# Adding an output bias to the residual on GpSimd instead of in TensorE's accumulators

## The chip, the cores and the metric

The kernel runs on one NeuronCore of a Trainium2 chip. The metric is device time of one execution in microseconds. TensorE (PE) multiplies, VectorE (DVE), ScalarE (ACT) and GpSimd (POOL) work element by element, and SyncE (SP) issues most transfers. The engines run their own instruction streams and meet at semaphores.

## What is computed

Two blocks on 256 tokens of width 1024. The first is a token mixer and a mixture of experts. The second, which the change touches, has four layers; layers 0 and 3 ("banded", kind 0) use sliding-window attention with biases, layer 1 a dilated one and layer 2 a block one, both without biases:

```python
for i in range(DEPTH_2):                       # 4 layers, kinds 0, 1, 2, 0
    kind, j = i % N_MIXERS, i // N_MIXERS
    if kind == 0:
        h = mixer_a(x, a_w_qkv[j], a_b_qkv[j], a_sinks[j], a_w_o[j], a_b_o[j], cos, sin)
    ...
    x = layer_norm(DN_ALPHA * x + h, ln_g[i, 0], ln_b[i, 0])
    x = layer_norm(DN_ALPHA * x + swiglu(x, w_gate_up[i], w_down[i]), ln_g[i, 1], ln_b[i, 1])

def mixer_a(x, w_qkv, b_qkv, sinks, w_o, b_o, cos, sin):
    ...
    return o.reshape(B, S, nq).astype(x.dtype) @ w_o + b_o
```

The bias in question is `b_o` (1024 numbers per banded layer), so that layer's first residual is ALPHA x + o w_o + b_o.

## The kernel before

x lies in SBUF as two token tiles of 128 rows and 1024 columns (`x[:, t, :]`, tile name `rs`). All weights stream from HBM through `ring` in units of 128x1024, each used once; ScalarE copies a unit to `high` (L1185) and VectorE subtracts to get `low` (L1654), both in the matmul's rounded fp32 type, so that each product is three matmuls (high x high, high x low, low x high). A unit is used on TensorE only when `low_done` has counted it.

A banded layer runs like this. TensorE turns x (L531) for the projections. It projects values, keys and four quads of queries, ScalarE takes each result out of PSUM (`pg`) and VectorE applies the rope (L2155 to L2159). Scores go to `pd`, VectorE masks them (L2175), ScalarE takes exponents (L1545), VectorE the reciprocal (L2201), and GpSimd multiplies them in (`weigh`, L369). `weighted_values` transposes (L1052 to L1054) and gathers; ScalarE writes the high part of the attention output (`oth`, L1558), VectorE the low part (`otl`, L2208, semaphore `otl_out`).

The output projection accumulates in the four banks of `pd`, one for each token tile and half of the columns. In a banded layer, four products of a row of ones and the bias row (L1128, fp32, each two instructions) open these accumulators; then `wo_part(n, t)` adds unit n (of 8) for tile t in six matmuls. Units 0 to 3 are done for both tiles, then come `weighted_values` for the third quad, units 4 and 5 for tile 0, `weighted_values` for the last quad, units 6 and 7 for tile 0 (semaphore `wo_first`), and units 4 to 7 for tile 1. VectorE, when `wo_first` has come, computes ALPHA x + `pd` (`residual`, L1960), statistics (L1964), and the normalisation (L1999, L2000), and TensorE turns the new x for the feed-forward.

`gb` holds two rows broadcast to all partitions. In a banded layer GpSimd first loads the bias into row 0 and the norm's offset into row 1 (L428, L429). When TensorE has used the bias (`bo_used`), GpSimd loads the norm's gain into row 0 (L380), between the third and the fourth `weigh`. Nearly all matmuls go through one helper, `mm` (L443), so the trace tells them apart by tile: `pd<-gb,ones` are the bias matmuls and `pd<-high,oth` and the like the projection.

## Time and profile before

| | |
|---|---|
| median of 3 runs | 2270.2 us (2267.29 to 2271.64) |
| the profiled execution | 2268.9 us, span 2267.1 us |
| TensorE busy | 2121.1 us (94%) |
| VectorE, ScalarE, GpSimd busy | 1281.1, 920.1, 109.2 us |
| mean granted TensorE clock | 0.969 |

Times in the trace count from the span's start. A row's "idle before" is the time its engine stood still ahead of it, with what released it. The granted clock is a share of TensorE's full speed: 1.00 is 2.4 GHz and 0.50 is 1.2 GHz. TensorE's matmuls overlap, so that one's duration is longer than the distance between two starts.

### The profile page before, as it was taken

The numbers are of one execution on the slowest core, as the hardware profiler recorded it, in microseconds if no ns is written. First come the engines' busy times: TensorE is split into PE (matmuls) and PEld (weight loads), VectorE is DVE, ScalarE is ACT, GpSimd is POOL, SyncE is SP. The second block draws the span as 40 slices with busy tenths as digits, with TensorE's granted clock in tenths as the row PEclk, the third lists the DMA queues.
The fourth block names the chain that finished last, engine by engine and source line by source line (L and its number), as shares of the span: only waits on it lengthen the run. The fifth ranks groups of instructions, "written<-read, shape, count | busy, mean of one in ns | idle before, by whom it ended". The sixth has DMA issues, their size and how long they took to land.

```text
span 2267.1 us, 27822 instructions
## 1 busy us (share of the span) xinstructions
PE 2121.1 (94%) x11438; PEld 1701.7 (75%) x11438; DVE 1281.1 (57%) x1890; ACT 920.1 (41%) x1452; POOL 109.2 (5%) x115
## 2 busy tenths in 40 slices
PE   6999999989999988999999998999998999988997
PEld 2468767857888775788898896788796788866886
DVE  3346723245555574655677784755685655747554
ACT  2233340015444444444335554444463544444442
POOL 1000000000000001000001111000011000020000
PEclk9999999999999998999999998999999999989999
DMA  8142444434555441555443441555443555423551
GB/s 348 39 185 78 178 149 148 185 121 167 186 186 186 167 168 66 185 186 184 163 174 131 149 149 57 186 186 185 168 149 112 186 186 186 168 77 145 183 182 74
DMA packets 47118, 357.36 MB, mean 158 GB/s; under 512 B 5370, under 2 KB 5541, under 8 KB 9680
## 3 DMA queue, kind: packets, MB, share of 16 engines
q1 hardware_dynamic: 41904, 336.61, 41.0%
q0 software_dynamic: 4800, 18.50, 2.4%
q8 instruction: 91, 1.49, 0.3%
q10 hardware_dynamic: 288, 0.47, 0.1%
q14 instruction: 35, 0.29, 0.0%
HBM read 354.51 MB, written 1.05 MB: 157 GB/s over the span
## 4 chain that ended last, share of the span: by engine, by line
PE 85%; DVE 9%; ACT 3%; issue 1%; DMA 1%; POOL 0%; SPq 0%; DVEq 0%; ACTq 0%
PE pg L443 55%; PE pd L443 24%; PE pm L443 2%; PE pm L908 1%; DVE small L1964 1%; DVE low L1654 1%; DMA ring<-in_wstream 1%; DVE rs L2000 1%; DVE rs L1999 1%; DVE rs L1960 1%; DVE ar L2175 1%; DVE ar L1758 1%; ACT ar L1545 1%; PE pm L1052 1%; DVE xs L2010 1%
## 5 line engine op out<-in xcount | busy, mean ns | idle before, releaser
L1654 DVE TENSOR_TENSOR low<-ring,high 128x1024 fp32r<-128x1024 f32 x512 | 622.8, 1236 | 355.2 <-ACT high L1185 354.9
L443 PE MATMUL pg<-high,xs 128*128 128x512 f32 (+1 forms) x2496 | 745.2, 376 | 24.8 <-DVE xs L2010 14.3
L1185 ACT CAST high<-ring 128x1024 fp32r<-128x1024 f32 x512 | 525.0, 1049 | 368.0 <-PE pd L443 165.5
L443 PEld LDWEIGHTS pg<-high,xs 128*128 128x128 f32 x2496 | 460.9, 193 | 113.9 <-issue 22.1
L443 PE MATMUL pg<-low,xs 128*128 128x512 f32 (+1 forms) x1248 | 465.6, 373 | 0.0
L443 PE MATMUL pd<-high,hid 128*128 128x512 f32 x960 | 311.7, 396 | 7.0 <-DVE hid L2089 7.0
L443 PEld LDWEIGHTS pg<-low,xs 128*128 128x128 f32 x1248 | 240.5, 193 | 40.4
L443 PE MATMUL pg<-xs,high 128*128 128x256 f32 x1344 | 242.0, 283 | 0.0
L443 PEld LDWEIGHTS pd<-high,hid 128*128 128x128 f32 x960 | 180.6, 188 | 50.5 <-DVE hid L2089 8.2
L443 PEld LDWEIGHTS pg<-xs,high 128*128 128x128 f32 x1344 | 206.0, 188 | 5.0 <-issue 4.7
L443 PE MATMUL pg<-rh,ring 128*128 128x256 f32 (+1 forms) x832 | 203.9, 404 | 0.0
L443 PEld LDWEIGHTS pg<-rh,ring 128*128 128x128 f32 x832 | 159.7, 194 | 42.6 <-issue 22.5
L443 PE MATMUL pd<-low,hid 128*128 128x512 f32 x480 | 189.5, 395 | 0.0
L443 PE MATMUL pg<-xs,low 128*128 128x256 f32 x672 | 189.1, 281 | 0.0
L443 PEld LDWEIGHTS pg<-xs,low 128*128 128x128 f32 x672 | 126.5, 188 | 0.0
L443 PEld LDWEIGHTS pd<-low,hid 128*128 128x128 f32 x480 | 90.3, 188 | 21.0
L369 POOL TENSOR_TENSOR ar<-ar,small 128x256 f32<-128x256 f32 (+1 forms) x64 | 82.9, 1323 | 433.1 <-DVE small L2201 432.9
L2089 DVE TENSOR_TENSOR hid<-pm,hid 128x512 fp32r<-128x512 f32 x60 | 41.5, 691 | 92.3 <-ACT hid L1477 92.3
L1477 ACT CAST hid<-pm 128x512 fp32r<-128x512 f32 x60 | 35.2, 586 | 124.0 <-PE pm L908 124.0
L1545 ACT ACTIVATE ar<-ar,small 128x257 f32<-128x257 f32 (+5 forms) x128 | 67.0, 525 | 41.5 <-DVE small L2195 30.1
L1486 ACT ACTIVATE ar<-pg 128x256 f32<-128x256 f32 x120 | 46.2, 386 | 84.5 <-PE pg L443 84.4
L2155 DVE TENSOR_TENSOR ar<-ar,ropes 128x512 f32<-128x512 f32 x42 | 36.9, 880 | 68.4 <-ACT ar L1524 42.7
(333 smaller groups left out, 2007.8 us busy)
## 6 DMA issues: line engine op xcount, KB each, us to landing
ring<-in_wstream SPq DMA_DIRECT2D x256, 1024.0 KB, 4.8
ring<-in_wstream SPq DMA_DIRECT2D x31, 2048.0 KB, 7.8
gb<-in_long_rows POOLq DMA_DIRECT2D x21, 512.0 KB, 4.6
hdec<-in_hy_decay POOLq DMA_DIRECT2D x4, 512.0 KB, 6.6
rh<-in_xt SPq DMA_DIRECT2D x1, 1024.0 KB, 11.8
rh<-in_ctx SPq DMA_DIRECT2D x1, 1024.0 KB, 20.1
cx<-in_cx_tables POOLq DMA_DIRECT2D x1, 1024.0 KB, 5.0
cx<-in_dft_tables POOLq DMA_DIRECT2D x1, 1024.0 KB, 8.6
```

Of the source, the lines that this page charges most:

```text
L369: last = gp.tensor_tensor(w, w, smx[:, b, 2, t, 2 * p:2 * p + 2].unsqueeze(2).to_broadcast([P, 2, n]), ALU.mult)
L443: ins = nc.tensor.matmul(dst, lhs, rhs, start=start, stop=stop, skip_group_check=skip)
L908: last = nc.tensor.transpose(pm[u % 2][:, i * T + t * P:i * T + (t + 1) * P], hidden[:, t, i * P:(i + 1) * P], ident)
L1052: nc.tensor.transpose(pm[i][:, 0:P], scores(q, 0)[:, h, g * P:(g + 1) * P], ident)
L1185: nc.scalar.copy(high[:, (s - split0) % NHIGH, :], ring[:, s % NRAW, :]).then_inc(S("high_done"), 1)
L1477: nc.scalar.copy(hid[:, u % 2, 0, :, :], pm[u % 2][:, :].rearrange("p (i t) -> p i t", t=T)).then_inc(S("hid_high"), 1)
L1486: nc.scalar.activation(silu_g[:, t, :], pg[t][:, 0:T], ACT.Silu).then_inc(S("silu_done"), 1)
L1545: last = nc.scalar.activation(s, s, ACT.Exp, bias=smx[:, b, 0, t, h:h + 1], accum_out=smx[:, b, 1, t, h:h + 1])
L1654: V.tensor_tensor(low[:, s % NRAW, :], ring[:, s % NRAW, :], high[:, (s - split0) % NHIGH, :].bitcast(F32), ALU.subtract).then_inc(S("low_ ...
L1758: last = V.scalar_tensor_tensor(d, src, w[i], d, ALU.mult, ALU.add)
L2089: V.tensor_tensor(hid[:, u % 2, 1, :, :], pm[u % 2][:, :].rearrange("p (i t) -> p i t", t=T), hid[:, u % 2, 0, :, :].bitcast(F32), ALU.sub ...
L2155: V.tensor_tensor(rt[:, 0, :, :], raw[:, e % 2, :, :], cos.unsqueeze(1).to_broadcast([P, 2, T]), ALU.mult)
```

## The change

In banded layers GpSimd, after the first loads and after TensorE has turned x, scales each token tile of x by ALPHA in place and adds the bias row, then loads the gain into `gb` row 0, all ahead of its first `weigh`. TensorE's bias matmuls go, and `wo_part` opens the accumulators itself. VectorE's residual there is a plain add. In all four layers `wo_first` is now signalled twice, behind unit 6 and behind unit 7, and VectorE waits for the one whose half it adds.

```diff
--- before.py
+++ after.py
@@ -373,11 +373,17 @@
             def attention(layer):
 
                 kind, q0 = KINDS[layer], 4 * layer
+                if kind == 0:
+                    gp.wait_ge(S("bo_landed"), 16 * (layer // 3 + 1))
+                    gp.wait_ge(S("x_turned"), 4 * (2 + 2 * layer))
+                    for t in range(TT):
+                        gp.tensor_scalar(x[:, t, :], x[:, t, :], ALPHA, None, ALU.mult).then_inc(S("x_raised"), 1)
+                        gp.wait_ge(S("x_raised"), 2 * (layer // 3) + t + 1)
+                        gp.tensor_tensor(x[:, t, :], x[:, t, :], gb[:, 0, :], ALU.add).then_inc(S("bo_added"), 1)
+                    gp.wait_ge(S("bo_added"), 2 * (layer // 3 + 1))
+                    gp.dma_start(gb[:, 0, :], row_of(f"ln_g{2 * layer}")).then_inc(S("gains_landed"), 16)
                 for i in range(3):
                     weigh(q0 + i)
-                if kind == 0:
-                    gp.wait_ge(S("bo_used"), layer // 3 + 1)
-                    gp.dma_start(gb[:, 0, :], row_of(f"ln_g{2 * layer}")).then_inc(S("gains_landed"), 16)
                 weigh(q0 + 3)
 
             gp.memset(cs[:, :, :], 0.0).then_inc(S("cs_zero"), 1)
@@ -1123,12 +1129,6 @@
 
                 n0 = first[("wo", layer)]
                 pe.wait_ge(S("masked"), PROJ[q0 + 4])
-                if kind == 0:
-                    pe.wait_ge(S("bo_landed"), 16 * (layer // 3 + 1))
-                    for t in range(TT):
-                        for c in range(2):
-                            last = mm(pd[:, 2 * t + c, :], ones[0:1, :], gb[0:1, 0, c * 512:(c + 1) * 512], True, False)
-                    last.then_inc(S("bo_used"), 1)
 
                 def wo_part(n, t):
                     w = weights(n0 + n)
@@ -1137,7 +1137,7 @@
                         for l, r in ((0, 0), (0, 1), (1, 0)):
                             o = (k % 2) * 512
                             last = mm(pd[:, 2 * t + c, :], (oth, otl)[l][:, k, t * P:(t + 1) * P], w[r][:, o:o + 512],
-                                      kind > 0 and k == 0 and (l, r) == (0, 0), k == KT - 1 and l == 1)
+                                      k == 0 and (l, r) == (0, 0), k == KT - 1 and l == 1)
                     return last
 
                 pe.wait_ge(S("otl_out"), q0 + 2)
@@ -1153,8 +1153,7 @@
                 weighted_values(q0 + 3)
                 pe.wait_ge(S("otl_out"), q0 + 4)
                 for n in (6, 7):
-                    last = wo_part(n, 0)
-                last.then_inc(S("wo_first"), 1)
+                    wo_part(n, 0).then_inc(S("wo_first"), 1)
                 for n in range(4, 8):
                     wo_part(n, 1).then_inc(S("unit_used"), 1)
                 at[0] = n0 + 8
@@ -1949,13 +1948,15 @@
                 then(V.tensor_tensor(mix[:, m, :], mix[:, m, :], mtmp[:, 0, :], ALU.add))
                 V.tensor_tensor(mix[:, m, :], mix[:, m, :], mtmp[:, 1, :], ALU.add).then_inc(S("mixed"), 1)
 
-            def residual(t, h, mod=None):
+            def residual(t, h, mod=None, raised=False):
 
                 half = x[:, t, h * 512:(h + 1) * 512]
                 src = pd[:, 2 * t + h, :]
                 if mod is not None:
                     then(V.tensor_tensor(rtmp, src, gb[:, mod, h * 512:(h + 1) * 512], ALU.mult))
                     ins = V.tensor_tensor(half, half, rtmp, ALU.add)
+                elif raised:
+                    ins = V.tensor_tensor(half, half, src, ALU.add)
                 else:
                     ins = V.scalar_tensor_tensor(half, half, ALPHA, src, ALU.mult, ALU.add)
                 ins.then_inc(S("res_out"), 1)
@@ -2282,15 +2283,17 @@
                 low_output(q0 + 3)
                 split_to(w0 + 11)
                 n = 3 + 2 * layer
-                dve.wait_ge(S("wo_first"), layer + 1)
-                residual(0, 0)
-                residual(0, 1)
+                if kind == 0:
+                    dve.wait_ge(S("bo_added"), 2 * (layer // 3 + 1))
+                for h in range(2):
+                    dve.wait_ge(S("wo_first"), 2 * layer + h + 1)
+                    residual(0, h, None, kind == 0)
                 statistics(n, 0, False)
                 normalised(n, 0)
                 dve.wait_ge(S("unit_used"), w0 + 8 - split0)
-                residual(1, 0)
+                residual(1, 0, None, kind == 0)
                 low_part(n, 0)
-                residual(1, 1)
+                residual(1, 1, None, kind == 0)
                 statistics(n, 1, False)
                 normalised(n, 1)
                 low_part(n, 1)
```

## Rows read from the trace of the kernel before

**Rows 1.** the page's part 4, the whole span's chain, its shares by engine.
```profile
PE 85%; DVE 9%; ACT 3%; issue 1%; DMA 1%; POOL 0%; SPq 0%; DVEq 0%; ACTq 0%
```

**Rows 2.** the chain in order of time, layer 0's projection (start, us, what).
```profile
867.72 16.49 PE pd L443 x56
```

**Rows 3.** timeline, layer 0's projection (start, us, engine, what, idle before it).
```profile
865.38 0.30 PE L1052 MATMUL pm<-consts,ar 128*128 128x128 f32 x1 [2.05 <-ACT ar L1556]
...
867.65 3.69 PE L443 MATMUL pd<-gb,ones 1*128 1x512 f32 x8
...
868.39 0.69 DVE L2208 TENSOR_TENSOR otl<-pg,oth 128x512 fp32r<-128x512 f32 x1 [1.93 <-ACT oth L1558]
...
871.28 0.50 PE L443 MATMUL pd<-high,oth 128*128 128x512 f32 x1
...
888.20 0.69 DVE L2208 TENSOR_TENSOR otl<-pg,oth 128x512 fp32r<-128x512 f32 x1 [16.12 <-ACT oth L1558]
...
888.95 0.51 PE L443 MATMUL pd<-high,oth 128*128 128x512 f32 x1 [1.41 <-DVE otl L2208]
```

**Rows 4.** the same timeline in layer 3.
```profile
2019.83 0.69 DVE L2208 TENSOR_TENSOR otl<-pg,oth 128x512 fp32r<-128x512 f32 x1 [3.32 <-ACT oth L1558]
...
2023.21 0.80 PE L443 MATMUL pd<-high,oth 128*128 128x512 f32 x1
```

**Rows 5.** TensorE by stretch (stretch, us, busy, instructions, granted clock, DMA, GB/s).
```profile
867.70:871.30 3.60, 3.60 (x11) 1.00 0.02 5
...
871.90:875.30 3.40, 3.40 (x10) 0.50 0.41 154
875.30:884.00 8.70, 8.70 (x39) 1.00 0.36 121
...
2015.30:2018.70 3.40, 3.40 (x18) 0.51 0.03 10
...
2023.20:2029.00 5.80, 5.80 (x15) 0.50 0.24 90
```

**Rows 6.** VectorE's residual (L1960) and the turn of tile 0 behind it (L531).
```profile
899.81 0.69 DVE L1960 SCALAR_TENSOR_TENSOR rs<-rs,pd 128x512 f32<-128x512 f32 x1 [0.51 <-PE pd L443]
...
  PE pd L443: 4.6, 8
...
907.12 0.66 PE L531 MATMUL pm<-consts,rs 128*128 128x128 f32 x4 [0.80 <-DVE rs L2000]
```

**Rows 7.** GpSimd's groups by shape (busy us, mean ns of one, idle before).
```profile
L369 POOL TENSOR_TENSOR ar<-ar,small 128x1536 f32<-128x1536 f32 x8 | 27.2, 3404 | 0.0
...
L395 POOL MEMSET rs<- 128x3684 f32 x1 | 3.2, 3168 | 23.1 <-PE pd L443 23.1
```

**Rows 8.** GpSimd and VectorE at the start of layer 0; L428's landing times.
```profile
806.08 0.53 POOL L428 DMA_DIRECT2D gb<-in_long_rows  x1 [302.34 <-DVE rs L1997]
...
DMA to landing us min/median/max: 3.9/4.0/4.0
...
813.61 2.36 DVE L1654 TENSOR_TENSOR low<-ring,high 128x1024 fp32r<-128x1024 f32 x2 [0.54 <-ACT high L1185]
...
818.81 0.69 DVE L2155 TENSOR_TENSOR ar<-ar,ropes 128x512 f32<-128x512 f32 x1 [2.84 <-ACT ar L1529]
...
824.51 0.69 DVE L2155 TENSOR_TENSOR ar<-ar,ropes 128x512 f32<-128x512 f32 x1 [1.34 <-ACT ar L1529]
...
830.20 0.69 DVE L2155 TENSOR_TENSOR ar<-ar,ropes 128x512 f32<-128x512 f32 x1 [1.33 <-ACT ar L1529]
...
846.46 3.17 POOL L369 TENSOR_TENSOR ar<-ar,small 128x256 f32<-128x256 f32 x4 [39.33 <-DVE small L2201]
```

**Rows 9.** GpSimd and VectorE side by side in layer 1.
```profile
1212.69 3.60 DVE L1654 TENSOR_TENSOR low<-ring,high 128x1024 fp32r<-128x1024 f32 x2
...
1216.21 3.23 DVE L2155 TENSOR_TENSOR ar<-ar,ropes 128x512 f32<-128x512 f32 x1
...
1212.85 6.05 POOL L369 TENSOR_TENSOR ar<-ar,small 128x768 f32<-128x768 f32 x2 [3.78 <-DVE small L2201]
```

## Prediction

> **What bounds the kernel now.** I read the page's chain that ended last first: 85% of the span is TensorE, 9% VectorE [rows 1]. So time is won by taking work off TensorE, or by shortening a wait that TensorE stands in, and work on another engine is free as long as it stays beside TensorE. Then I followed the chain in order of time through layer 0's output projection: it runs through one unbroken stretch of 56 matmuls into `pd`, 16.49 us long [rows 2]. Eight of those 56 are the bias matmuls that the change removes; the other 48 are units 0 to 3 of the projection (four units, two token tiles, six matmuls each). GpSimd is not on that chain. Four views then carry the numbers: the timeline at the bias matmuls of layers 0 and 3 (what would TensorE wait for without them?), the granted clock by stretch around them, VectorE's idle time ahead of its residual, and what VectorE and GpSimd do to each other when both are busy.
>
> **Bias matmuls removed: the start of the projection.** In layer 0 the first bias matmul starts at 867.65 and the first projection matmul at 871.28 [rows 3]. The whole 3.63 us is not won. The projection also waits for VectorE's low half of the attention output (`otl_out`), which starts at 868.39, takes 0.69 and so ends at 869.08 [rows 3]. Where TensorE has nothing else to do it starts 0.06 after such an end (888.20 + 0.69 = 888.89, matmul at 888.95) [rows 3]. So the new start is 869.15 and the gain 2.13 us. TensorE stands idle for about 1.4 us instead. Layer 3: the same operation ends at 2019.83 + 0.69 = 2020.52, the new start is 2020.59 against 2023.21 [rows 4], gain 2.62 us. Together 4.75 us. `wo_part` now opens the accumulators itself with the start flag, which is no instruction. The wait on `bo_landed` leaves TensorE; it was long satisfied.
>
> **Bias matmuls removed: the clock.** The bias matmuls contract over a single row. The granted clock is 1.00 while they run in layer 0 (867.70 to 871.30), 0.50, the 1.2 GHz level, from 871.90 to 875.30, directly behind them, and 1.00 again from 875.30 [rows 5]. In layer 3 they also run at 1.00 and the projection behind them at 0.50 from 2023.20 to 2029.00 [rows 5]. What the engine did before each fall was to stream those single-row matmuls, though the trace counts it as busy. I take it that they let the clock fall as idling would, and that an idle gap of 1.4 us with full matmuls behind it does less harm than 3.6 us of them: in layer 0 the gap of 2.05 us before 865.38 [rows 3] had no fall behind it (1.00 from 867.70 on). It is no law: layer 3 is at 0.51 from 2015.30 to 2018.70, behind the same gap [rows 5]. A stretch at 0.50 does half the work of its length, so the two cost 3.4 / 2 = 1.7 us and 5.8 / 2 = 2.9 us, together 4.6 us. Bounds: 0 (it falls all the same) to 4.6. Since the clock moves with what lies around it and everything behind layer 0 shifts, I count one new stretch of 1.7 us at 0.50 somewhere and keep 2.9 us.
>
> **`wo_first` in two steps, all four layers.** VectorE may add the first half of tile 0 when unit 6 is done, not unit 7. In layer 0 it stood idle for 0.51 us before that add, waiting for TensorE [rows 6]; ahead of that it converts the last two weight units and can't be earlier. The add and its statistics then run beside unit 7's six matmuls, and the second half starts 0.5 us sooner. The idle time put down to TensorE ahead of this line is 4.6 us in 8 waits [rows 6]: one at the projection and one at the end of each of the four layers, and the change leaves the latter alone. I take the 0.51 for all four projections. The saving reaches TensorE, since it stands idle 0.80 us before the second turn of tile 0 for VectorE's normalisation [rows 6]. 4 x 0.51 = 2.0 us, bounds 1.3 (if the first turn, where it can gain only about 0.3, decided) to 2.0.
>
> **Work added on GpSimd.** Per banded layer two scalings and two adds, each 128x1024 f32. None of that size is in the trace. The adds: its multiplication takes 3.40 us at 128x1536 [rows 7], in proportion 3.40 x 1024 / 1536 = 2.3 us each. The scaling, one tensor in, is bounded below by a memset, 3.17 us for 3684 columns, so 0.9 us for 1024 [rows 7], and above by the add, 2.3; I take 1.2, near the memset, since its second operand is a constant. Per layer 2 x (1.2 + 2.3) = 7.0 us, bounds 6.4 to 9.2. GpSimd starts when `a_bo` has landed: issued at 806.08, about 4.0 to land [rows 8], so at 810.1, and ends near 817 to 821. The turns that read x are over by then. Queued behind it on GpSimd are the DMA of the gain (now in place some 50 us sooner, moved ahead of three `weigh` calls) and the first `weigh`, which before started at 846.46 [rows 8]. So 25 us of cover. Cost on GpSimd's own queue: nothing. Its `weigh` of the last quad no longer waits for TensorE; nobody was waiting for it.
>
> **What it does to VectorE.** In layer 1, with GpSimd at two multiplications for 6.05 us, VectorE's rope product took 3.23 us instead of 0.69, and two weight conversions 3.60 instead of 2.36 [rows 8, 9]. So VectorE lost 3.78 us in 6.05, or 0.62 per us of GpSimd's time. The Trainium skill, "SBUF — State Buffer", section "Who interferes with whom", says why: a VectorE instruction with two inputs in SBUF shares GpSimd's read interface, and the one that comes second waits for the whole of the other. The trace agrees: each of those instructions has two SBUF inputs. For this change 0.62 x 7.0 = 4.4 us of VectorE's time per banded layer, 5.7 at the upper bound. VectorE's idle time from there on is 0.54 + 2.84 + 1.34 + 1.33 = 6.05 us up to the rope at 830.20 [rows 8]. One projection of a quad lasts 824.51 - 818.81 = 5.70 us there, in which VectorE converts two units (2.36), so TensorE's units come with time in hand. So I cost it at 0, bounds 0 to 2 us per layer (the loss in one lump just before 818.81). If that cover were gone the price would be the 4.4. The same page gives no duration; the Trainium skill, "GPSIMD Engine Reference", section "2.1 Instruction dispatch", adds about 6 us for the first call of freshly loaded code. No run here shows it. By it GpSimd would end near 827, still 19 us before its next work, and the sum would stay.
>
> The residual itself becomes an add instead of a scale-and-add, with one input in PSUM as before: 0, both are one pass over 512 columns.
>
> **Sum.** 4.75 + 2.9 + 2.0 = 9.65 us. The profiled execution took 2268.9 us (span 2267.1), so 2259.3. It lies 1.3 us under the median of the three runs, 2270.2; against that the forecast is 2260.5.
>
> **Rivals.**
> (A) The clock falls all the same, since TensorE now idles for 1.4 us right behind the small gather matmuls. For: in layer 3 the clock is at 0.50 already in the stage before. Against: the projection begins 2.1 to 2.6 us sooner with full matmuls. Gain 4.75 + 2.0 = 6.8, time 2263.4. Chance 0.22.
> (B) GpSimd's work isn't hidden: VectorE's delay passes the idle time and reaches the score chain from 830 on, which has none to spare. 2 us per layer off the sum: gain 5.7, time 2264.5. With (A) as well, gain 2.8, time 2267.4. Together 0.13.
> (C) Slower. GpSimd's one-input scaling runs far above my bound, and each us of it takes 0.62 from VectorE. Per layer the loss must pass 6.05 us idle plus half of the 9.65 gain, 10.9 us, so GpSimd must be busy for 17.6 us per layer, or 6.5 us for each scaling; at 10 us each it is (24.6 x 0.62 - 6.05) x 2 - 9.65 = +8.8 us, time 2279. By the rows an operation on one input has no reason to cost thrice one on two. Chance 0.03.
> (D) The change doesn't do what it says: TensorE's saved time turns up as a wait for something later than `otl_out`, for instance converted weight units. Against: VectorE, which converts them, is idle for 16.12 us in that stage [rows 3], so all that could be converted was. Time 2269 or so. Chance 0.04.
> Forecast: 0.58.
>
> **Range and chances.** 80%: 2256.5 (both clock stretches kept, 4.6) to 2266.0 (A and B, part of their joint case left out). A measurement of this kernel can tell about 0.2%, 4.5 us, from no change, so faster means under 2265.7. That holds for the forecast, A, and B alone: 0.86. Same: B with A, and D, and a little of the spread: 0.11. Slower: C, 0.03.
>
> **What would show it.** Right: the first projection matmul starts 0.06 us after `otl`; no matmuls from `gb`; the granted clock is 1.00 over most of the 48 matmuls, which then take some 11 us; the 0.51 us idle before the residual is gone in all four layers; GpSimd's four operations at the start of layers 0 and 3 take 6.4 to 9.2 us in all, VectorE's conversions and ropes beside them are stretched, and TensorE has no new wait before 830. Wrong: the clock at 0.50 in the projection; TensorE waiting on VectorE in the projections of q or k; GpSimd's scaling above 2.3 us.

## The result, and the profile after

| | before | after |
|---|---|---|
| median of the runs made together (4 each) | 2268.74 us | 2254.91 us (2253.15 to 2257.61) |
| the profiled execution | 2268.9 us, span 2267.1 | 2257.61 us, span 2255.8 |
| TensorE busy | 2121.1 us | 2106.3 us |
| VectorE, ScalarE, GpSimd busy | 1281.1, 920.1, 109.2 us | 1291.1, 920.1, 133.6 us |

The ratio is 0.9939, with a 95% interval of 0.9922 to 0.9956: faster by 13.8 us. The forecast was 2260.5, with a range of 2256.5 to 2266.0. The direction was right, but the time lies 1.6 us under the range. So two questions are left: which term was too small, and whether the rest belongs to the change.

The page's part 4 of after, the chain's shares by engine, against [rows 1]:

```profile
PE 83%; DVE 10%; ACT 4%; issue 2%; DMA 1%; POOL 0%; SPq 0%; ACTq 0%; DVEq 0%
```

TensorE still bounds the kernel and GpSimd is still not on the chain, though it works 24 us longer. TensorE's timeline of after at layer 0's projection (start, us, engine, what, idle before it), against [rows 3]:

```profile
868.47 1.56 PE L449 MATMUL pg<-ar 128*64 128x256 f32 x16
871.49 0.47 PE L449 MATMUL pd<-high,oth 128*128 128x512 f32 x1 [1.46 <-issue]
...
2014.60 0.47 PE L449 MATMUL pd<-high,oth 128*128 128x512 f32 x1 [1.46 <-issue]
```

The last row is the projection's start in layer 3. VectorE's timeline in layer 0:

```profile
870.70 0.69 DVE L2209 TENSOR_TENSOR otl<-pg,oth 128x512 fp32r<-128x512 f32 x1 [1.93 <-ACT oth L1557]
```

Where eight bias matmuls ran, TensorE is idle for 1.46 us, in layer 3 as in layer 0, and the projection starts 0.10 us after VectorE's low half (870.70 + 0.69 = 871.39). The times are not those of [rows 3], since the execution before this point was 2.2 us longer, so from here on distances are compared. The granted clock around it, TensorE by stretch (stretch, us, busy, instructions, granted clock, DMA, GB/s), against [rows 5]; the last three rows are layer 3:

```profile
867.70:871.30 3.60, 2.33 (x22) 1.00 0.00 0
871.60:875.30 3.70, 3.70 (x17) 1.00 0.02 4
875.30:882.60 7.30, 7.30 (x33) 1.00 0.44 144
...
2014.60:2018.60 4.00, 4.00 (x17) 1.00 0.00 0
2018.70:2023.00 4.30, 4.30 (x20) 1.00 0.32 99
2023.20:2029.00 5.80, 5.47 (x40) 1.00 0.58 192
```

No stretch of either projection is at 0.50, the 1.2 GHz level. TensorE is less busy right ahead of the projection than before (2.33 of 3.60 us instead of 3.60), and the clock nonetheless stays at its 2.4 GHz level.

The last term, VectorE's first residual in layer 0, and the answer on the line of the residual for the other layers and the feed-forwards (idle time, times), against [rows 6]:

```profile
895.54 2.36 DVE L1653 TENSOR_TENSOR low<-ring,high 128x1024 fp32r<-128x1024 f32 x2 [0.25 <-ACT high L1184]
897.82 0.68 DVE L1959 TENSOR_TENSOR rs<-rs,pd 128x512 f32<-128x512 f32 x1
...
  PE pd L449: 2.6, 4
```

The 0.51 us of idle time is gone. Of 4.6 us in 8 waits, 2.6 us in 4 are left. But the residual now starts right behind the conversion of two weight units: what is late next is VectorE's own order of work.

GpSimd at the start of layer 0, against [rows 7] and [rows 8]:

```profile
813.20 3.77 POOL L380 TENSOR_SCALAR rs<-rs 128x1024 f32<-128x1024 f32 x1 [3.40 <-DMA gb<-in_long_rows]
817.05 2.64 POOL L382 TENSOR_TENSOR rs<-rs,gb 128x1024 f32<-128x1024 f32 x1
819.67 3.74 POOL L380 TENSOR_SCALAR rs<-rs 128x1024 f32<-128x1024 f32 x1
823.50 2.39 POOL L382 TENSOR_TENSOR rs<-rs,gb 128x1024 f32<-128x1024 f32 x1
...
848.77 1.60 POOL L369 TENSOR_TENSOR ar<-ar,small 128x256 f32<-128x256 f32 x2 [21.97 <-DVE small L2202]
```

The four operations take 3.77 + 2.64 + 3.74 + 2.39 = 12.5 us, not 7.0, and lie outside the bounds of 6.4 to 9.2. GpSimd still has 22 us of idle time before its first `weigh`. The 6 us that the prediction allowed for a first call didn't show: the first scaling started when the bias had landed and took 3.77 us, the second 3.74. VectorE beside it:

```profile
810.83 9.95 DVE L1653 TENSOR_TENSOR low<-ring,high 128x1024 fp32r<-128x1024 f32 x6 [0.32 <-ACT high L1184]
821.11 1.11 DVE L2156 TENSOR_TENSOR ar<-ar,ropes 128x512 f32<-128x512 f32 x1 [0.33 <-ACT ar L1528]
...
823.53 4.57 DVE L1653 TENSOR_TENSOR low<-ring,high 128x1024 fp32r<-128x1024 f32 x2
```

Undisturbed, two conversions take 2.36 us and the rope product 0.69 [rows 8]. So VectorE lost (9.95 - 3 x 2.36) + (1.11 - 0.69) + (4.57 - 2.36) = 5.5 us in 12.5, 0.44 per us of GpSimd instead of 0.62. The idle time ahead of these rows, 0.54, 2.84 and so on before, is down to 0.3 us each: the loss went into VectorE's idle time.

The table gives distances between starts of TensorE's matmuls, in us, for each kernel of the study. "Start" runs from the turn of tile 1 to the first projection matmul (in layers 0 and 3), "48" over the 48 matmuls of units 0 to 3 and the weighted values behind them, up to unit 4 (in after the 48 matmuls alone take 11.2 us of it), "end" from unit 6 to the turn of tile 0, "turns" from there to the turn of tile 1 in layer 0, "layer 1" from its turn of tile 1 to the first projection matmul and from there to unit 6.

| kernel | start 0 | 48 in 0 | end 0 | turns 0 | layer 1 | start 3 | 48 in 3 |
|---|---|---|---|---|---|---|---|
| before | 65.66 | 17.67 | 8.93 | 10.61 | 273.63 + 28.06 | 67.74 | 18.76 |
| after | 63.65 | 16.07 | 8.44 | 10.50 | 273.79 + 25.31 | 65.05 | 16.08 |
| e1 after again | 63.63 | 16.07 | 8.43 | 10.55 | 273.82 + 25.31 | 65.08 | 16.08 |
| e2 no bias | 63.63 | 16.07 | 8.94 | 10.60 | 273.78 + 27.85 | 64.95 | 16.07 |
| e3 full rows | 65.19 | 16.40 | 8.94 | 9.09 | 273.52 + 28.02 | 66.63 | 16.40 |
| e4 two steps | 65.79 | 17.59 | 8.44 | 10.53 | 273.63 + 28.04 | 67.20 | 17.67 |
| e5 GpSimd later | 67.47 | 16.08 | 8.43 | 8.96 | 276.50 + 27.90 | 69.01 | 16.07 |
| e6 GpSimd last | 65.16 | 16.07 | 8.44 | 10.52 | 273.86 + 25.30 | 64.98 | 16.08 |
| e7 no bias, two steps | 63.63 | 16.08 | 8.44 | 10.52 | 275.25 + 26.88 | 65.10 | 16.07 |
| e8 high first | 63.57 | 15.56 | 8.97 | 10.48 | 273.81 + 24.79 | 64.41 | 15.56 |
| e9 GpSimd long | 67.52 | 16.06 | 8.44 | 10.52 | 273.75 + 27.86 | 69.11 | 16.07 |
| e10 VectorE's order | 65.15 | 16.08 | 8.43 | 8.69 | 276.28 + 25.30 | 65.12 | 16.08 |
| e11 both orders | 62.05 | 15.56 | 8.46 | 8.87 | 276.28 + 24.78 | 64.42 | 15.57 |

From before to after the three terms of the sum are: start 65.66 - 63.65 = 2.01 and 67.74 - 65.05 = 2.69, together 4.70; clock 17.67 - 16.07 = 1.60 and 18.76 - 16.08 = 2.68, together 4.28; two steps 8.93 - 8.44 = 0.49, and about 0.50 in each of the other three layers, 2.0. That makes 11.0 us, or a ratio of 0.9951. It is within the measured interval, yet in layer 1, whose work on TensorE up to there is the same, the second part differs too, by 28.06 - 25.31 = 2.75 us. The distance between the two turns differs with the clock as well. It is 10.5 us where the granted clock over it is 0.84, and 9.0 where it is 1.00; in after it is 10.50, 8.97, 8.97 and 10.52 in layers 0 to 3, in before 10.61, 10.54, 9.08 and 10.62.

### The profile page after: what moved, and what is told of

It is laid out like the page before. It is cut to its first block, busy times and chain, and to the rows that moved or that the text cites. A ratio compares the mean times of both kernels' runs of the same rounds, so it can differ in the third digit from the quotient of the medians.

```text
span 2255.8 us, 27800 instructions
## 1 busy us (share of the span) xinstructions
PE 2106.3 (93%) x11422; PEld 1690.1 (75%) x11422; DVE 1291.1 (57%) x1890; ACT 920.1 (41%) x1452; POOL 133.6 (6%) x123
## 4 chain that ended last, share of the span: by engine, by line
PE 83%; DVE 10%; ACT 4%; issue 2%; DMA 1%; POOL 0%; SPq 0%; ACTq 0%; DVEq 0%
PE pg L449 55%; PE pd L449 23%; PE pm L449 2%; DVE low L1653 1%; PE pm L914 1%; DVE small L1965 1%; DVE rs L2001 1%; DVE rs L2000 1%; DMA ring<-in_wstream 1%; DVE ar L2176 1%; DVE rs L1961 1%; DVE ar L1757 1%; ACT high L1184 1%; ACT ar L1544 1%; PE pm L1058 1%
## 5 line engine op out<-in xcount | busy, mean ns | idle before, releaser
L1653 DVE TENSOR_TENSOR low<-ring,high 128x1024 fp32r<-128x1024 f32 x512 | 630.8, 1252 | 356.0 <-ACT high L1184 355.7
L449 PEld LDWEIGHTS pg<-high,xs 128*128 128x128 f32 x2496 | 458.2, 191 | 114.5 <-issue 21.7
```

What stands on the lines that cost most here:

```text
L449: ins = nc.tensor.matmul(dst, lhs, rhs, start=start, stop=stop, skip_group_check=skip)
L1653: V.tensor_tensor(low[:, s % NRAW, :], ring[:, s % NRAW, :], high[:, (s - split0) % NHIGH, :].bitcast(F32), ALU.subtract).then_inc(S("low_ ...
```

## The experiments

Each diff is against before or after, as said. The expectations stand as they were written ahead of the runs. The numbers are those of the table (e1 is the first experiment); the ninth is told ahead of the eighth.

### The changed kernel once more

No edit. The question is whether the time beyond the forecast comes again.

> The changed kernel as it is, for a second profile and a closer ratio. The first profile won 13.5 us from the first turn of layer 0 on: 11.0 us by the terms of my sum (4.7 start, 4.3 clock, 2.0 two steps) and 4.3 us in layer 1 (2.75 in its output projection, 1.6 at the turn behind it), where only the clock differed, less some given back elsewhere. Theory 1 (the clock's share in layer 1 is chance): the second profile has other places at 0.50, the terms of the sum measure 11 us again, and the ratio settles near 0.995 (2268.7 - 11 = 2257.7). Theory 2 (it is brought about by the change): layer 1's projection is at 1.00 again and the ratio stays at 0.9939.

Measured: 2254.17 us (2252.97 to 2255.56), ratio 0.9944 (0.9931 to 0.9957). The stretches of the table are those of the first profile within 0.05 us, layer 1's 25.31 among them. So the time is the kernel's own and not one lucky execution. One stretch outside the table is not the same: the turns of layer 3 are 8.96 us apart here and 10.52 in the first profile, so the clock can differ between two executions of one program. What the ratio can't say is whether all of it comes from the change's parts; the others below can.

### The bias left out, nothing else

Against before; the output bias is missing from the result, and GpSimd does nothing new.

```diff
-                    gp.wait_ge(S("bo_used"), layer // 3 + 1)
+                    gp.wait_ge(S("bo_landed"), 16 * (layer // 3 + 1))
...
-                            last = mm(pd[:, 2 * t + c, :], ones[0:1, :], gb[0:1, 0, c * 512:(c + 1) * 512], True, False)
...
-                                      kind > 0 and k == 0 and (l, r) == (0, 0), k == KT - 1 and l == 1)
+                                      k == 0 and (l, r) == (0, 0), k == KT - 1 and l == 1)
```

> The kernel before without the eight bias matmuls of each banded layer and with nothing in their place; the output bias is left out of the result. wo_first stays one signal, GpSimd adds nothing. My theory: the projection starts 2.1 and 2.6 us sooner, 0.06 us behind otl, and stays at a clock of 1.00, which gives 4.3 more: 9.0 us, 2259.7, ratio 0.9960. Rival A (the clock falls all the same while TensorE idles): 4.75 us, 2264.0, ratio 0.9979. Against the changed kernel it shows what GpSimd's work costs: 11.0 less 9.0 less 2.0 for the two steps, so nothing by my theory.

Measured: 2257.26 us, ratio 0.9958 (0.9942 to 0.9973), where 0.9960 was expected. "Start" falls by 2.03 and 2.79, "48" by 1.60 and 2.69: removing the bias matmuls gives 9.1 us by itself, and the start and clock terms are both theirs. (Layer 1 is 301.6 us here, as in before; what it gives in after is missing.)

### The same bias matmuls over all 128 rows

Against before: a stationary identity and the bias in all rows of `gb`. The arithmetic is the same, the number of instructions too.

```diff
-                            last = mm(pd[:, 2 * t + c, :], ones[0:1, :], gb[0:1, 0, c * 512:(c + 1) * 512], True, False)
+                            last = mm(pd[:, 2 * t + c, :], ident, gb[:, 0, c * 512:(c + 1) * 512], True, False)
```

> The kernel before, its bias matmuls with the identity as stationary operand and all 128 rows of the broadcast bias: same number, same columns, same type, all rows of the array instead of one. My theory (it is the single row that lets the clock fall): the bias matmuls take the same 3.6 us, the projection starts at the same place, but at a clock of 1.00 in both banded layers; 4.3 us won, 2264.4, ratio 0.9981. Rival (the clock falls for what lies ahead of them, the small transposes and gathers, or for their fp32 type): 0.50 behind them as before, ratio 1.000.

Measured: 2262.25 us, ratio 0.9978 (0.9967 to 0.9989); 0.9981 was expected, 1.000 by the rival. TensorE's timeline and its granted clock by stretch, of this kernel:

```profile
870.02 3.70 PE L443 MATMUL pd<-gb,consts 128*128 128x512 f32 x8
873.15 0.79 PE L443 MATMUL pd<-high,oth 128*128 128x512 f32 x1
...
867.70:871.30 3.60, 3.55 (x25) 1.00 0.02 5
871.60:875.30 3.70, 3.70 (x13) 1.00 0.00 0
875.30:882.60 7.30, 7.30 (x34) 1.00 0.48 174
...
2018.70:2023.00 4.30, 4.30 (x16) 1.00 0.09 25
2023.20:2029.00 5.80, 5.80 (x27) 1.00 0.37 121
```

The eight matmuls take 3.70 us as they did with a single row (3.69 in [rows 3]). But the projection behind them runs at 1.00, and "48" is 16.40 us in both layers instead of 17.67 and 18.76. The fourth experiment below keeps the single row and has the fall in both layers (17.59 and 17.67); the eight profiles that have 1.46 us of idle time in this place have none of it in 16 of 16. So the fall of the clock belongs to the single-row matmuls: the number of instructions, their columns and their time are unchanged (the stationary operand is an identity in place of ones as well, which no run varies by itself). That is 1.27 + 2.36 = 3.6 us of the clock term without removing an instruction; "start" is shorter too, by 0.47 and 1.11, the larger in layer 3, where the stage ahead ran at 0.51 before [rows 5]. The measured gain, 0.22%, is 5.0.

### The first residual in two steps, nothing else

Against before.

```diff
-                    last = wo_part(n, 0)
-                last.then_inc(S("wo_first"), 1)
+                    wo_part(n, 0).then_inc(S("wo_first"), 1)
...
-                dve.wait_ge(S("wo_first"), layer + 1)
-                residual(0, 0)
-                residual(0, 1)
+                for h in range(2):
+                    dve.wait_ge(S("wo_first"), 2 * layer + h + 1)
+                    residual(0, h)
```

> The kernel before with wo_first signalled behind unit 6 and behind unit 7, and nothing else. My theory: VectorE's 0.51 us idle ahead of the residual goes in four layers, and the turns behind it come 0.5 us sooner each: 2.0 us, 2266.7, ratio 0.9991. Rival (the turn of the first half waits for TensorE's own matmuls): 0.3 us in each layer, 1.3 us, ratio 0.9994. The distance from otl to the second turn in the profile tells them apart more closely than the times.

Measured: 2264.55 us, ratio 0.9991 (0.998 to 1.0002), as expected but not told from 1 by the time alone. The trace tells it: "end" is 8.44 in place of 8.93.

### GpSimd's work behind the first `weigh`

Against after. The same four operations and DMA, some 35 us later.

```diff
+                weigh(q0)
                 if kind == 0:
...
-                for i in range(3):
+                for i in (1, 2):
                     weigh(q0 + i)
```

> The changed kernel with GpSimd's scaling and add behind the first weigh of a banded layer, where VectorE's mask, maximum and rope steps are on the chain, instead of ahead of it. In the changed kernel's profile that work takes 12.5 us per layer (scaling 3.8, add 2.6 each), not my 7.0, and VectorE lost 5.6 us beside it, 0.45 us per us. My theory (it is free only where VectorE has idle time and GpSimd nothing due): the second weigh, due some 12 us behind the first, comes 4 us late, and VectorE loses up to 5.6 us on the chain: 3 to 6 us per banded layer, 6 to 12 us in all, ratio to the kernel before 0.997 to 1.000. Rival (GpSimd's place does not matter): 0.9944, as the changed kernel.

Measured: 2263.41 us, ratio 0.9978 (0.9967 to 0.999): the gain is more than halved. GpSimd, then VectorE, of this kernel in layer 0:

```profile
849.57 2.77 POOL L381 TENSOR_SCALAR rs<-rs 128x1024 f32<-128x1024 f32 x1
852.42 2.34 POOL L383 TENSOR_TENSOR rs<-rs,gb 128x1024 f32<-128x1024 f32 x1
854.74 3.21 POOL L381 TENSOR_SCALAR rs<-rs 128x1024 f32<-128x1024 f32 x1
858.03 2.87 POOL L383 TENSOR_TENSOR rs<-rs,gb 128x1024 f32<-128x1024 f32 x1
...
853.73 1.58 DVE L2157 TENSOR_TENSOR ar<-ar,ropes 128x512 f32<-128x512 f32 x1 [3.64 <-ACT ar L1529]
855.24 1.25 DVE L2158 SCALAR_TENSOR_TENSOR ar<-ar,ropes 128x256 f32<-128x256 f32 x1
...
857.47 4.51 DVE L1654 TENSOR_TENSOR low<-ring,high 128x1024 fp32r<-128x1024 f32 x2
```

Here the rope products (1.58 and 1.25 us) and the conversions (4.51 instead of 2.36) lie on the way to the scores, and VectorE's loss passes to TensorE: "start" is 3.82 us longer than in after in layer 0 and 3.96 in layer 3. Of each, 2.7 to 2.8 us are idle time of TensorE, the rest is its matmuls at a lower clock (0.53 and 0.57 from 8 to 4 us ahead of the projection, where after has 1.00 and 0.99). The 7.8 us together are close to the 8.5 by which the medians differ, but that hides more: in the profiles layer 1 is 5.3 us longer than in after (304.4 and 299.1) and layer 2 3.1 us shorter, in code that neither kernel changes. Rival B's mechanism is real; its place was wrong.

### GpSimd's work behind the last `weigh`

Against after: the `weigh` loop of all four quads is moved ahead of the block.

```diff
+                for i in range(4):
+                    weigh(q0 + i)
                 if kind == 0:
...
-                for i in range(3):
-                    weigh(q0 + i)
-                weigh(q0 + 3)
```

> The changed kernel with GpSimd's scaling and add behind the last weigh, beside the output projection, where VectorE has stood idle for 12 to 16 us. It measures the scaling without VectorE beside it. Theory 1 (my 1.2 us was right and the port shared with VectorE stretched it to 3.8): the scaling takes 1.0 to 1.5 us here, the add 2.3. Theory 2 (GpSimd's scaling is that slow by itself): 2.9 us or more. Either way it ends before the residual needs it, and the ratio is the changed kernel's, 0.9944 within 0.001.

Measured: 2253.54 us, ratio 0.9946 (0.9934 to 0.9958). GpSimd has nobody beside it here, so this is also the price of its operations alone. Its timeline in layer 0, and the answer on the scaling's line (min/median/max ns):

```profile
876.39 2.77 POOL L382 TENSOR_SCALAR rs<-rs 128x1024 f32<-128x1024 f32 x1
879.25 2.40 POOL L384 TENSOR_TENSOR rs<-rs,gb 128x1024 f32<-128x1024 f32 x1
...
L382 POOL TENSOR_SCALAR rs<-rs x4: 2768/2770/2773, 876.4 to 2020.9; 128x1024 f32<-128x1024 f32 x4
```

The scaling takes 2.77 us every time. So it is slow by itself, slower than the add of two tensors of that size (2.40), and sharing with VectorE adds 0.35 to 1.0 us (3.12 to 3.77 in after). The late place is as good as the early one. One stretch is worse, and GpSimd is not the cause of it: "start" in layer 0 is 65.16 instead of 63.65. The tenth experiment has it too (65.15), whose code up to there is that of after. TensorE's transposes ahead of the projection, first of after, then of the tenth:

```profile
867.69 0.30 PE L1058 MATMUL pm<-consts,ar 128*128 128x128 f32 x1 [2.38 <-ACT ar L1555]
```

```profile
866.09 0.40 PE L1058 MATMUL pm<-consts,ar 128*128 128x128 f32 x1 [1.84 <-ACT ar L1555]
...
871.47 0.48 PE L449 MATMUL pd<-high,oth 128*128 128x512 f32 x1 [1.46 <-issue]
```

From the first transpose to the projection it is 3.80 us in the one (to 871.49, above) and 5.38 in the other, and the transpose itself takes 0.30 and 0.40. From 860 to 870 the granted clock was 0.84 in after and 0.69 in the tenth. The same code runs there at another clock.

### The bias left out and the two steps: the change without GpSimd's work

Against before, the diffs of the second and the fourth experiment together; the output bias is missing.

> The kernel before without the bias matmuls and with wo_first in two steps; GpSimd does nothing for the bias, which is left out of the result. It is the changed kernel less GpSimd's work. My theory (that work is hidden): 11.0 us by the terms, ratio 0.9951, the same as the changed kernel within the interval. Rival (GpSimd's work costs TensorE time at the start of the banded layers): this kernel is the faster by up to 4 us, ratio 0.993 or less. The stretch from the turn of layer 0 to its first projection matmul, 63.65 us in the changed kernel, would be shorter here by the same.

Measured: 2255.16 us, ratio 0.995 (0.9939 to 0.9962), 0.9951 expected. Taking all of GpSimd's 25 us away brings nothing over after (0.9939 and 0.9944), and "start" is the same within 0.05 us (63.63 and 65.10 against 63.65 and 65.05). GpSimd's work costs nothing where the change put it. Layer 1 takes 275.25 + 26.88 = 302.1 us here, where before takes 301.7 and after 299.1.

### Three scalings where one is

Against after: two more scalings by 1.0 per tile, so that GpSimd is busy 23.8 us per layer. This is rival C's case, made on purpose.

```diff
-                        gp.tensor_scalar(x[:, t, :], x[:, t, :], ALPHA, None, ALU.mult).then_inc(S("x_raised"), 1)
-                        gp.wait_ge(S("x_raised"), 2 * (layer // 3) + t + 1)
+                        for i in range(3):
+                            gp.tensor_scalar(x[:, t, :], x[:, t, :], ALPHA if i == 2 else 1.0, None, ALU.mult).then_inc(S("x_raised"), 1)
+                            gp.wait_ge(S("x_raised"), 6 * (layer // 3) + 3 * t + i + 1)
```

> The changed kernel with three scalings of each tile on GpSimd instead of one (two of them by 1.0), so that its work per banded layer grows from 12.5 us to about 25. It asks where the cover ends and what a us beyond it costs, which is the price of my slower rival (C). By the prediction's rate, 0.62 us of VectorE per us of GpSimd less 6.05 us of idle time: 9.2 us per layer beyond the changed kernel, 18 in all, ratio 1.002 to the kernel before. By the rate of the changed kernel's profile, 0.45: 5 us per layer, 10 in all, 0.9988. If the idle time of VectorE up to the mask step hides it all: 0.9944.

Measured: 2264.34 us, ratio 0.9986 (0.9976 to 0.9995). By a rate of 0.45 it was to be 0.9988, by the 0.62 of the prediction 1.002. GpSimd and VectorE in layer 0:

```profile
812.74 9.35 POOL L381 TENSOR_SCALAR rs<-rs 128x1024 f32<-128x1024 f32 x3 [3.15 <-DMA gb<-in_long_rows]
822.18 2.69 POOL L383 TENSOR_TENSOR rs<-rs,gb 128x1024 f32<-128x1024 f32 x1
824.95 9.07 POOL L381 TENSOR_SCALAR rs<-rs 128x1024 f32<-128x1024 f32 x3
834.10 2.64 POOL L383 TENSOR_TENSOR rs<-rs,gb 128x1024 f32<-128x1024 f32 x1
...
834.42 2.88 DVE L2157 TENSOR_TENSOR ar<-ar,ropes 128x512 f32<-128x512 f32 x1
```

The rope at the head of the score chain waits inside GpSimd's last add (2.88 us instead of 0.69), and "start" grows by 3.87 and 4.06 us. Together that is 7.9 us of the 10 that the rate of 0.45 gives; that the ratio came so close is partly chance, since layers 1 and 2 again differ from after by 2.5 us more and 3.1 less. Some 11 us more of GpSimd in a layer cost 4 us there, so the cover of [rows 8] ends between 12.5 and 23.8 us of GpSimd's work.

### The projection's high parts first

Against after: at units 4 and 6 TensorE starts with the high part of the attention output, which ScalarE has ready before VectorE's low half; units 0 and 1 no longer wait for the second quad.

```diff
-                    for k in (2 * i, 2 * i + 1):
-                        for l, r in ((0, 0), (0, 1), (1, 0)):
+                    if opens:
+                        pe.wait_ge(S("oth_out"), q0 + i + 1)
+                    for l, r in ((0, 0), (0, 1), (1, 0)):
+                        if opens and l:
+                            pe.wait_ge(S("otl_out"), q0 + i + 1)
+                        for k in (2 * i, 2 * i + 1):
...
-                pe.wait_ge(S("otl_out"), q0 + 2)
+                pe.wait_ge(S("otl_out"), q0 + 1)
                 for n in range(4):
+                    if n == 2:
+                        pe.wait_ge(S("otl_out"), q0 + 2)
...
```

> The changed kernel with the output projection ordered so that TensorE waits less for the low half of the attention output: units 0 and 1, which need only the first quad, start without the second; and where a quad's first unit opens, the four matmuls with the high half run while VectorE makes the low half. My theory: the 1.4 us idle ahead of the projection in the two banded layers goes (2.8 us), and each of the eight waits of 1.41 us ahead of units 4 and 6 falls to 0.7 (5.6 us), together 8.4 us below the changed kernel, ratio to the kernel before 0.9907. Rival (VectorE's or ScalarE's later steps are then due and the turns behind the projection come no sooner): half of it, 0.9925.

Measured: 2252.23 us, ratio 0.9943 (0.9929 to 0.9958). Neither 0.9907 nor the rival's 0.9925 was met. TensorE's wait ahead of units 4 and 6 did get shorter (0.78 us instead of 1.41). TensorE's, then VectorE's timeline of this kernel:

```profile
883.02 0.70 PE L449 MATMUL pd<-high,oth 128*128 128x512 f32 x2 [0.78 <-ACT oth L1561]
...
890.99 2.36 DVE L1657 TENSOR_TENSOR low<-ring,high 128x1024 fp32r<-128x1024 f32 x2 [0.26 <-ACT high L1188]
893.27 0.68 DVE L1963 TENSOR_TENSOR rs<-rs,pd 128x512 f32<-128x512 f32 x1
```

The residual stands behind two conversions, as in after, and unit 6 being done sooner doesn't help it: "end" goes back from 8.44 to 8.97. In layer 1 the second part is 0.52 us shorter and "end" takes all of it back; in the banded layers 0.5 us of some 1.2 to 1.8 goes. The rest of the missing gain is not explained by this wait. In this profile the turns of layer 2 also stand 11.87 us apart at a clock of 0.71, where after has 8.97 at 1.00.

### VectorE's order around the residual

Against after: one of the two conversions is moved behind work that TensorE waits for.

```diff
-                split_to(w0 + 11)
+                split_to(w0 + 10)
...
                 low_part(n, 0)
+                split_to(w0 + 11)
```

> The changed kernel with VectorE converting only one of the last two weight units ahead of the residual and the other behind the low half of tile 0. In the profiles VectorE starts the residual 0.0 us behind the second conversion, so it is what stands ahead now. Theory: the residual starts up to 1.1 us sooner, held by unit 6 of the projection; the second turn's idle 0.75 us goes, in four layers: 3.0 us below the changed kernel, ratio 0.9931. Rival (TensorE is still busy with the projection of tile 1 then, and the late conversion delays tile 1's residual): no change, 0.9944.

Measured: 2251.58 us (2248.33 to 2252.29), ratio 0.9929 (0.9917 to 0.994); 0.9931 expected. "Turns" falls from 10.50 to 8.69. Most of that is the clock. TensorE over the turns of after in layers 0 and 1, then of this kernel in layer 0:

```profile
903.78:914.28 10.50, 8.45 (x33) 0.84 0.40 162
1417.18:1426.14 8.96, 6.92 (x33) 1.00 0.47 191
```

```profile
903.77:912.46 8.69, 7.06 (x33) 1.00 0.48 184
```

At the same clock of 1.00 the order of VectorE's work gives 0.28 us per layer, 1.1 in four, and not the 3.0 expected. The other 1.5 us each in layers 0 and 3 come from the clock. Both kernels with this order have all eight of their turns at 1.00, and the seven others with the two steps and the old order of VectorE and TensorE have 14 of 28 there, so the order may well be what keeps the clock up; no run isolates it. That the ratio came out as expected doesn't show that the reason was right.

### Both orders together

The edits of the last two experiments in one kernel.

> The order of e8 and the order of e10 together on the changed kernel. In e8 TensorE was 1.3 us per layer sooner at unit 6 but the turn came 8.97 us behind it instead of 8.44, since VectorE stood between. Theory: with VectorE's conversion out of the way the turn comes 8.35 us behind unit 6 and its second half without idle time: 5 to 8 us below the changed kernel, ratio 0.991 to 0.9925. Rival: the end of the projection is bound by the low half of the last quad alone, and it is e8's ratio, 0.9943.

Measured: 2246.17 us (2242.88 to 2248.34), ratio 0.9906 (0.9892 to 0.992). VectorE and TensorE in layer 0:

```profile
890.80 1.23 DVE L1657 TENSOR_TENSOR low<-ring,high 128x1024 fp32r<-128x1024 f32 x1 [0.26 <-ACT high L1188]
891.95 0.68 DVE L1963 TENSOR_TENSOR rs<-rs,pd 128x512 f32<-128x512 f32 x1
...
898.43 0.60 PE L537 MATMUL pm<-consts,rs 128*128 128x128 f32 x4
899.25 0.66 PE L537 MATMUL pm<-consts,rs 128*128 128x128 f32 x4 [0.22 <-DVE rs L2005]
```

One conversion instead of two stands ahead of the residual, "end" is back at 8.46, and the turns are 8.87 us apart in all four layers. By the ratios to before this version is 0.33% faster than the changed kernel, and faster than either reordering alone. How much of it is shorter waits and how much the clock, no run separates.

## Why the prediction was right and wrong

**The start of the projection: right.** 4.75 us forecast, 4.70 measured. The rule that carried it (the new start is the end of VectorE's low half plus what TensorE needs to begin) held within 0.04 us, and rival D, in which the time turns up as another wait, is refuted by the same rows. The runs add a condition: the sixth and tenth experiments, with the start in the same place, lose 1.5 us of this term again in layer 0, by the clock of the stage before.

**The clock: this is the step that failed.** The cause was named rightly, as the third experiment shows, and rival A is refuted: 1.46 us of idle time ahead of the projection left the clock at 1.00 in both layers. The size was wrong. The rows gave 1.7 + 2.9 = 4.6 us, and then "one new stretch of 1.7 us at 0.50 somewhere" was taken off, so that 2.9 was counted. Measured: 4.28 in the two projections. The deducted stretch had no row behind it: the prediction put the clock of everything else at a cost of 1.7 us, and in after it was a gain. In layer 1, in code that the change leaves alone, it gave 2.75 us in the projection and about 1.5 between the turns. Such a new stretch does exist in other kernels (the 1.5 us of the sixth and tenth experiments), but after doesn't have it.

**Two steps: right.** 4 x 0.50 = 2.0 us, in each layer. That VectorE's conversions stood ahead of the residual was seen in the prediction. That they set its start once the wait is gone was not followed up; it cost this forecast nothing, and the eighth and tenth experiments turn on it.

**GpSimd's work: the cost of zero was right, its terms were not.** The scaling was put at 1.2 us, "near the memset, since its second operand is a constant". It takes 2.77 alone and 3.1 to 3.8 beside VectorE; so "scaling above 2.3 us", named as a sign against the prediction, came true. The rate at which VectorE loses was too high (0.44, not 0.62), so that VectorE's loss was 5.5 us per layer and not 4.4, still under the 6.05 us of idle time. The two errors partly cancelled, which is luck: 12.5 us at the rate of 0.62 would have been 7.8. The Trainium skill, "GPSIMD Engine Reference", section "4.1 Engine selection", says that operations with two inputs are about twice slower on GpSimd than on VectorE and those with one input roughly at line rate. The traces agree with the first part (2.40 us for the add, where VectorE's subtraction of two tensors of that size has a mean of 1.25). They contradict the second: 2.77 us for the scaling, more than for the add. Rival B's mechanism holds 35 us later (fifth experiment) and rival C's was measured at 23.8 us of GpSimd per layer: 4 us lost there, where C's working gives 23.8 x 0.62 - 6.05 = 8.7. C put the point from which the whole gain is gone at 17.6 us per layer; at 23.8 a part of it (0.14%) was still left.

**From the sum to the time.** The terms as measured give 4.70 + 4.28 + 2.0 = 11.0 us, where 9.65 was counted: 1.35 us of the 5.6 by which the forecast missed. Another 1.45 us come from the reference: the median of before was 2270.2 in the runs ahead of the prediction and 2268.7 with the runs of after (2266.0 to 2267.8 in later ones), and the 1.3 us added for the profiled execution's place under that median only raised the forecast. By the sum as measured the time would have been 2270.2 - 11.0 = 2259.2, inside the range. The other 2.8 us lie outside the terms. From the turn of tile 1 in layer 0 on, the profile of after is 13.5 us shorter than that of before: 11.0 by the terms, 4.2 in layer 1 besides, and 1.9 given back in the feed-forwards. Granted clock of TensorE in the same stretch of layer 1, of before, after and the fifth experiment, in this order:

```profile
1380.00:1390.00 10.00, 8.00 (x45) 0.50 0.01 2
```

```profile
1380.00:1390.00 10.00, 8.00 (x44) 0.90 0.01 2
```

```profile
1380.00:1390.00 10.00, 7.61 (x43) 0.50 0.01 2
```

The stretches are the same time from each span's start, and the three kernels are within 2.2 us of each other where layer 1 starts. The fifth experiment has the code of after in this layer and the clock of before. Over the eleven profiles whose kernels leave the order of work in it alone, the whole stretch of layer 1 takes 299.1 to 304.4 us. It came again in a second profile of the same program (25.31 and 25.31 in after), and moves when something far ahead is moved, in either direction. Layer 2 does the same: 114.5 us to its unit 6 in before, 114.6 in after, and 111.4 to 111.5 in the fourth to seventh and the ninth experiments. So part of the 13.8 us is no property of the bias's new place, and an equal change elsewhere could lose it. The experiment without GpSimd's work has none of layer 1's gain (302.1 against 301.7 in before) and a ratio of 0.995, which is what the sum as measured gives; in its profile layer 2 is 3.0 us shorter than in before, though. What decides where the clock falls in layer 1 stays open; no run isolates it.

**The range.** It took in the clock's terms that the change touches: both stretches kept give 2258.8. Down to the bound of 2256.5 that leaves 2.3 us for every stretch that the change doesn't touch. Layer 1's alone spread over 5.3 us here. With 2 to 3 us more on each side it would have held the time.

## What to carry to other kernels

A matmul over one row cost TensorE here the time of one over 128, and also the clock of the matmuls behind it; before moving such a bias elsewhere, the same instruction with an identity and full rows is a one-line try. Ask of work for GpSimd whether VectorE has idle time in the same microseconds: the same four operations were free in the two places where it had, and cost 8 us in a third, where VectorE's work was next on the way to the scores. When a wait gets shorter, look at once at what the waiting engine had queued ahead of it, since two edits that gave nothing and 0.1% here gave 0.33% together. And compare stretches in several builds before a few us are put down to a cause: untouched layers moved by 3 to 5 us here with the clock alone.

## What the runs showed of the hardware that was not expected

- Eight single-row matmuls and eight over 128 rows take the same 3.7 us and are counted as busy alike. Behind the first the granted clock is 0.50 (the 1.2 GHz level), in both layers of before and of the fourth experiment; behind the second it is 1.00 (2.4 GHz), in both layers of the third.
- An idle gap of 1.46 us with the small gather matmuls before it did not lower the clock behind it, in both banded layers of eight profiles. But the same code came out at different clocks in different kernels: by 1.5 us in layer 0's scores (after and the tenth experiment) and by 5.3 us in layer 1 (after and the fifth).
- GpSimd's scaling of 128x1024 by a constant takes 2.77 us, more than its add of two tensors (2.40), and up to 3.77 beside VectorE's two-input operations.
- VectorE loses 0.44 us per us of GpSimd's work in its conversions and ropes, in after; the multiplications of [rows 9] cost it 0.62.
